# An expert-weight ring of 2 MB slots, and small matmuls packed in row and column groups, in a decoder step with 32 experts

## The reference

```
def moe(h, router_w, router_b, w_gu, b_gu, w_d, b_d):
    tok = h.reshape(-1, D_MODEL)
    logits = tok @ router_w + router_b
    top_v, top_i = lax.top_k(logits, TOP_K)            # 4 of 32 experts
    gates = scatter(softmax(top_v), top_i)             # (tokens, 32)
    for each expert:                                   # wgu 1024x2048, wd 1024x1024
        u = tok @ wgu + bgu
        glu = minimum(u[:, ::2], 7.0)
        lin = clip(u[:, 1::2], -7.0, 7.0)
        a = glu * sigmoid(1.702 * glu) * (lin + 1.0)
        acc += g[:, None] * (a @ wd + bd)
    return acc
```

## Time and profile before

| what | value |
|---|---|
| median of 3 runs | 1356.5 us (1354.03 to 1365.93) |
| span of the profiled execution | 1356.6 us |
| PE busy | 1267.8 us, 93% |
| VectorE / ScalarE / GpSimd busy | 317.1 / 256.0 / 67.5 us |
| moved by DMA | 500.45 MB, mean 369 GB/s |
| loads of w_gate_up | 256 of 1024 KB, 9.2 us from issue to landing (median) |
| loads of w_down | 128 of 1024 KB, 9.4 us |
| late constants | 1 of 288 KB, 11.6 us |

### The profile page before, as it was taken

The page is one execution under the profiler, slowest core; times in us unless marked ns, Lnnn a source line. Parts: engine busy times, 40 slices in busy tenths (PEclk is TensorE's granted clock), DMA queues, the critical chain, the costliest instruction groups (busy, mean ns, idle before and its releaser), DMA issues.

```text
span 1356.6 us, 20869 instructions
## 1 busy us (share of the span) xinstructions
PE 1267.8 (93%) x7744; PEld 606.1 (45%) x7744; DVE 317.1 (23%) x558; ACT 256.0 (19%) x573; POOL 67.5 (5%) x81
## 2 busy tenths in 40 slices
PE   7999988999799999999999999999999999999997
PEld 3588744454634343443434344343434344343433
DVE  1144525135411112211111122211111122111113
ACT  3143331222301011111201010211101011111102
POOL 2021003312000000000000000000000000000000
PEclk8999999999799999999999999999999999999999
DMA  9489978987889999999999999999999999999980
GB/s 338 171 316 353 338 251 295 354 305 226 332 329 405 413 411 415 418 415 417 415 417 409 411 419 414 419 415 416 409 417 413 415 420 416 419 403 416 415 340 36
DMA packets 120784, 500.45 MB, mean 369 GB/s; under 512 B 11925, under 2 KB 12074, under 8 KB 87946
## 3 DMA queue, kind: packets, MB, share of 16 engines
q1 hardware_dynamic: 117226, 488.03, 90.7%
q0 software_dynamic: 3520, 11.93, 2.5%
HBM read 495.20 MB, written 4.72 MB: 369 GB/s over the span
## 4 chain that ended last, share of the span: by engine, by line
PE 84%; DVE 5%; DMA 4%; issue 3%; ACT 3%; SPq 1%; POOL 0%; DVEq 0%; ACTq 0%; POOLq 0%
PE psum L838 32%; PE psum L865 17%; PE psum L798 7%; PE psum L424 6%; PE psum L411 5%; PE psum L813 5%; PE psum L827 4%; ACT arena L909 2%; PE psum L506 2%; SPq L386 1%; PE psum L549 1%; DVE arena L1496 1%; DMA arena<-cache_k 1%; DMA arena<-cache_v 1%; DMA arena<-x_sample 1%
## 5 line engine op out<-in xcount | busy, mean ns | idle before, releaser
L838 PE MATMUL psum<-arena 128*64 128x512 f32 x2048 | 445.3, 592 | 0.0
L838 PEld LDWEIGHTS psum<-arena 128*64 128x64 f32 x2048 | 161.0, 137 | 278.5 <-issue 278.5
L865 PE MATMUL psum<-arena 128*64 128x512 f32 x1024 | 226.8, 595 | 22.7 <-issue 11.7
L909 ACT ACTIVATE arena<-psum 128x512 f32<-128x512 f32 (+4 forms) x234 | 122.7, 545 | 532.7 <-PE psum L865 197.6
L1475 DVE TENSOR_SCALAR arena<-psum 128x512 f32<-128x512 f32 x32 | 22.1, 692 | 735.4 <-PE psum L838 735.4
L865 PEld LDWEIGHTS psum<-arena 128*64 128x64 f32 x1024 | 77.6, 137 | 151.3 <-issue 136.5
L813 PE MATMUL psum<-arena 128*128 128x512 f32 (+1 forms) x204 | 98.6, 612 | 25.6 <-DVE arena L1496 24.4
L1104 ACT ACTIVATE arena<-arena 128x512 f32<-128x512 f32 x32 | 20.1, 630 | 460.2 <-DVE arena L1475 460.2
L424 PE MATMUL psum<-arena 128*128 128x512 f32 x224 | 101.3, 610 | 3.4 <-DMA arena<-w_in 3.4
L411 PE MATMUL psum<-arena 128*128 128x128 f32 (+2 forms) x693 | 87.8, 279 | 15.1 <-DMA arena<-ret_norm_g 6.6
L798 PEld LDWEIGHTS psum<-arena 128*128 128x128 f32 x816 | 94.8, 196 | 14.2 <-issue 13.0
(11 more groups left out here) (195 smaller groups left out, 563.0 us busy)
## 6 DMA issues: line engine op xcount, KB each, us to landing
arena<-w_gate_up SPq DMA_DIRECT2D x256, 1024.0 KB, 9.2
arena<-w_down SPq DMA_DIRECT2D x128, 1024.0 KB, 9.4
arena<-cache_v SPq DMA_DIRECT2D x128, 256.0 KB, 5.1
arena<-cache_k SPq DMA_DIRECT2D x96, 256.0 KB, 5.8
arena<-w_in SPq DMA_DIRECT2D x7, 2048.0 KB, 10.7
arena<-cache_k POOLq DMA_DIRECT2D x32, 256.0 KB, 5.7
arena<-w_out SPq DMA_DIRECT2D x2, 2048.0 KB, 10.7
out<-arena POOLq DMA_DIRECT2D x1, 2048.0 KB, 13.5
```

Source lines behind the costliest of these rows:

```text
L838: last = mm(psum[64 * g:64 * (g + 1), b, :], xt[:, k, lhs], w[:, c:c + 512], start=False, stop=k == KC - 1, skip_group_check=True)
L865: last = mm(psum[64 * g:64 * (g + 1), 2, :], at_sb[:, q, SLOTS * half:SLOTS * (half + 1)], dn[:, m, 512 * g:512 * (g + 1)], start=m == 0, ...
L909: return nc.scalar.activation(out, in_, ACT.Copy, scale=scale)
```

## The change

The weights of an expert come in six parts of 2 MB, four of gate-up (256 rows each) and two of down (512 rows each). A part is laid out so that each partition holds 2 or 4 neighbouring rows of DRAM, one run of 16 KB. The parts go in turn through a ring of eight slots (16 MB), wherever their places lie in the arena (`PLACE`); one counter `w_used` releases them. To find room, the small buffers of the expert stage move to other regions. Since a partition now holds neighbouring rows, the gather picks every second column of the normed tokens, its gains come in a matching order through two more small transposes, and the transposes of the activation take every fourth column.

Four kinds of small matmuls are arranged anew. The bias table stands on 64 partitions, one half of each 1024 columns on 32 rows, and a bias matmul works on 32 rows and 64 columns of the array. The sample part of the combine becomes one unit of four matmuls of 32 columns and 256 elements into one bank, added to a buffer `y_quarters`, which is filled ahead of the loop and copied back after it. In the gather, the sample tile is kept twice, on partitions 0 to 31 and 32 to 63 (with its ranks), and its matmuls use 32 rows each, for two banks in turn. The last pair does not gather; pairs of the second loop gather for themselves. The first loads ahead of the loop are issued in another order. (Long blocks of removed lines are cut; they stand in the functions above.)

```diff
+RING = 8
+WSLOT = 4096
+PLACE = (0, 6, 7, 4, 5, 3, 1, 2)
+PARTS = 6
...
+    put("expert", np.tile(np.eye(E), (P // E, 1)))
...
-        gu = at(0, KC, F2)
+        gate_slot = [at(WSLOT * place, 2, F2) for place in PLACE]
+        down_slot = [at(WSLOT * place, 4, D) for place in PLACE]
-        dn = at(DN, KC, D)
...
-            pe.wait_ge(gains_in, 48)
-            transposes(V, [gain_in[0:20, :]], 20)
+            pe.wait_ge(gains_in, 64)
+            V.wait_empty(pe)
+            tr(psum[:, V.bank(), 0:20], gain_in[0:20, :], ident[0:20, 0:20])
+            for m in range(2):
+                last = tr(psum[:, V.bank(), 20 + 4 * m:24 + 4 * m], gain2_in[0:4, m::2], ident[0:4, 0:4])
+            V.filled(last)
...
-                for k in range(KC):
...
+                for kk in range(2):
+                    for m in range(2):
+                        for bank in range(2):
+                            cols = slice(512 * bank + 256 * kk + m, 512 * bank + 256 * (kk + 1), 2)
+                            o = psum[:, 6 + bank, P * (2 * kk + m):P * (2 * kk + m + 1)]
+                            for tile in range(2):
+                                mm(o, hn[:, tile, cols], sel[:, tile].rearrange("p a b -> p (a b)"),
+                                   start=tile == 0, stop=False, skip_group_check=True)
+                        for bank in range(2):
+                            cols = slice(512 * bank + 256 * kk + m, 512 * bank + 256 * (kk + 1), 2)
+                            o = psum[:, 6 + bank, P * (2 * kk + m):P * (2 * kk + m + 1)]
+                            rows = slice(NS * bank, NS * (bank + 1))
+                            last = mm(o, hn[rows, 2, cols], sel[rows, 2].rearrange("p a b -> p (a b)"),
+                                      start=False, stop=True, skip_group_check=True)
                 last.then_inc(xt_full, 1)

             def combine(m):

                 pe.wait_ge(sgt_ready, m + 1)
                 pe.wait_ge(out_ready, m * 2 + 1)
+                for u in range(4):
+                    tile, half = u // 2, u % 2
+                    if u >= 2:
+                        pe.wait_ge(comb_added, m * 5 + (u - 1))
+                    mm(psum[:, 3 + half, :], sgt[:, P * tile:P * (tile + 1)],
+                       out2[:, 512 * half:512 * (half + 1)], start=True, stop=True)\
+                        .then_inc(comb_full, 1)
+                pe.wait_ge(comb_added, m * 5 + 3)
+                for j in range(4):
+                    last = mm(psum[NS * j:NS * (j + 1), 3, 0:256], sgt[:, 2 * P:2 * P + NS],
+                              out2[:, 256 * j:256 * (j + 1)], start=True, stop=True)
+                last.then_inc(comb_full, 1)
+
+            def combine_last(m):
...
+                pe.wait_ge(comb_added, m * 5)
...
-            def pair(n, ahead):
-
-                pe.wait_ge(xt_ready, n + (1 if ahead else 2))
-                pe.wait_ge(esel_ready, n + (1 if ahead else 2))
+            def pair(n, landed, ahead):
+
+                pe.wait_ge(xt_ready, n + 1)
+                pe.wait_ge(esel_ready, n + 1)
                 for e in range(2):
                     pe.wait_ge(u_read, n * 2 + (e + 1))
                     lhs = slice(SLOTS * e, SLOTS * (e + 1))
-                    for b in range(2):
...
+                    for b, g in ((0, 0), (1, 1), (0, 1), (1, 0)):
+                        mm(psum[64 * g:64 * (g + 1), b, :], esel[E * b:E * (b + 1), e, :],
+                           bgu[E * b:E * (b + 1), g, :], start=True, stop=False, skip_group_check=True)
+                    for kk in range(4):
+                        slot, value = landed(PARTS * e + kk)
+                        pe.wait_ge(wt_in[slot], value)
+                        for m in range(2):
+                            for b in range(2):
+                                for g in range(2):
+                                    c = 1024 * g + 512 * b
+                                    last = mm(psum[64 * g:64 * (g + 1), b, :], xt[:, 2 * kk + m, lhs],
+                                              gate_slot[slot][:, m, c:c + 512], start=False,
+                                              stop=kk == 3 and m == 1, skip_group_check=True)
+                        last.then_inc(w_used, 1)
...
+                    for m in range(4):
+                        last = tr(psum[:, 5, P * m:P * (m + 1)], a_sb[:, m::4], ident)
                     last.then_inc(at_full, 1)
                     if e == 1:
-                        pe.wait_ge(comb_added, n * 6 + 6)
+                        pe.wait_ge(comb_added, n * 5 + 5)
...
-                    for m in range(KC):
...
+                    for q in range(2):
+                        slot, value = landed(PARTS * e + 4 + q)
+                        pe.wait_ge(wt_in[slot], value)
+                        for m in range(4):
+                            for g in range(2):
+                                last = mm(psum[64 * g:64 * (g + 1), 2, :],
+                                          at_sb[:, m, SLOTS * q:SLOTS * (q + 1)],
+                                          down_slot[slot][:, m, 512 * g:512 * (g + 1)],
+                                          start=q == 0 and m == 0, stop=q == 1 and m == 3)
+                        last.then_inc(w_used, 1)
+
+            pe.wait_ge(hn_copied, 1)
...
+            with pe.Fori(0, PAIRS // 2 - 1) as i:
+                pair(i * 2, in_turn(i, 0), True)
+                pair(i * 2 + 1, in_turn(i, 1), True)
+            pair(PAIRS - 2, in_turn(PAIRS // 2 - 1, 0), True)
+            pair(PAIRS - 1, in_turn(PAIRS // 2 - 1, 1), False)
...
+            act.wait_ge(hn_ready, 2)
+            copy(hn[NS:2 * NS, 2, :], hn[0:NS, 2, :]).then_inc(hn_copied, 1)
...
+            v.tensor_copy(rankm[NS:2 * NS, 2, 0:E], rankm[0:NS, 2, 0:E]).then_inc(rank_ready, 1)
+            dve.wait_ge(rank_ready, 2)
...
-                v.tensor_copy(esel, ident[:, bass.ds(first, 2)].unsqueeze(2).broadcast_to([P, 2, SLOTS]))\
+                v.tensor_copy(esel[0:2 * E], late_const("expert")[0:2 * E, bass.ds(first, 2)].unsqueeze(2)
+                              .broadcast_to([2 * E, 2, SLOTS]))\
...
+            def added(n):
+                for i in range(5):
+                    tile, half = i // 2, i % 2
+                    dve.wait_ge(comb_full, n * 5 + (i + 1))
+                    if i < 4:
+                        dst, got = y[:, tile, 512 * half:512 * (half + 1)], psum[:, 3 + half, :]
+                    else:
+                        dst, got = y_quarters, psum[:, 3, 0:256]
+                    v.tensor_tensor(dst, got, dst, ALU.add).then_inc(comb_added, 1)
...
+            dve.wait_ge(y_ready, 2)
+            for j in range(4):
+                v.tensor_copy(y_quarters[NS * j:NS * (j + 1), :], y[0:NS, 2, 256 * j:256 * (j + 1)])\
+                    .then_inc(quarters_ready, 1)
+            dve.wait_ge(quarters_ready, 4)
...
+            dve.wait_ge(comb_added, more * 5 + 5 * PAIRS)
+            for j in range(4):
+                v.tensor_copy(y[0:NS, 2, 256 * j:256 * (j + 1)], y_quarters[NS * j:NS * (j + 1), :])\
+                    .then_inc(quarters_ready, 1)
+            dve.wait_ge(quarters_ready, 8)
...
-            g_.memset(bgu, 0.0)
-            g_.memset(sgt, 0.0)
             link(g_.memset(out2, 0.0))
             pool.sem_inc(moe_zero, 1)
             pool.wait_ge(*mark["w_out"])
+            g_.memset(sgt, 0.0)
...
+            def load_part(e, part, slot):
+                if part < 4:
+                    src = w_gu[e] if isinstance(e, int) else w_gu[bass.ds(e, 1)].rearrange("a d f -> (a d) f")
+                    src, dst = src[256 * part:256 * (part + 1), :], gate_slot[slot]
                 else:
+                    src = w_dn[e] if isinstance(e, int) else w_dn[bass.ds(e, 1)].rearrange("a d f -> (a d) f")
+                    src, dst = src[512 * (part - 4):512 * (part - 3), :], down_slot[slot]
+                sp.dma_start(dst, src.rearrange("(p m) n -> p m n", p=P)).then_inc(wt_in[slot], 16)
+
+            def load_turn(t):
+                load_part(t // PARTS, t % PARTS, t % RING)

             sp.wait_ge(*mark["block6"])
+            load_turn(0)
             sp.wait_ge(rot_done, 2)
             sp.dma_start(rw, t["router_w"][0].rearrange("(k p) e -> p k e", p=P)).then_inc(router_in, 16)
             sp.dma_start(rb, t["router_b"][0:1].partition_broadcast(P).rearrange("p a e -> p (a e)"))\
@@ -1739,61 +1805,43 @@
             sp.dma_start(y[:, 0:2, :], x_p).then_inc(y_in, 16)
             sp.dma_start(y[0:NS, 2, :], x_s).then_inc(y_in, 16)
             sp.dma_start(f_gain, t["final_norm_g"].partition_broadcast(P)).then_inc(fg_in, 16)
+            sp.wait_ge(v_used, 32)
+            load_turn(1)
+            load_turn(2)
             sp.wait_ge(st2_ready, 1)
             sp.dma_start(late, t["shape_consts"][:, ncols:ncols + late_cols]).then_inc(late_in, 16)
+            sp.wait_ge(ret_ready, 1)
+            sp.wait_ge(*mark["vblk3"])
```

(72 more changed lines are left out.)

151 lines of the change are left out of this document (37 added, 114 removed).

## The result

| kernel | median | ratio to before |
|---|---|---|
| before | 1359.2 us (1354.03 to 1365.93, 4 runs) | 1 |
| changed | 1343.98 us (1341.97 to 1345.02, 4 runs) | 0.9887 [0.9866, 0.9908] |

The change makes the kernel 1.1% faster; a ratio of 1 lies outside the interval. The profiled execution spans 1343.2 us against 1356.6, 13.4 less; the forecast was 23 less. The rows are read in the order of those of before.

What follows compares the result with a forecast made beforehand. TensorE, busy 93% of the span, was taken as the bound, with DMA a few per cent behind. 1356.6 - 15.4 - 20.6 + 8.9 - 2.8 + 4.4 + 2.3 = 1333.4 us; own range 1322 to 1345, overall 1297 to 1376.

Steps and rivals of the forecast that it cites:

- Unit prices: TensorE: a full 512-column record takes 0.43 us, column groups overlap almost without loss, each change of array shape costs 0.19 us.
- Bias: 32 bias blocks, four matmuls at a time on 32 rows: 1.72 us becomes 1.24, gaining 15.4 us.
- Sample combine: Sample part of 16 combines, packed four matmuls at a time: 1.29 us saved each, gaining 20.6 us.
- Gather: 15 gathers in the loop: packing makes 5.55 us into 6.14, losing 8.9 us; the stride of two costs nothing.
- No last gather: Last pair: without its gather the transposes start when the activations are ready, gaining 2.8 us, not 5.55.
- Before the loop: Stretch ahead of the loop: first gather +0.9 us, copies on VectorE +1.2; sum +2.3, ends +1 and +8.
- DMA: Weight loads in 16 KB runs reach 427 GB/s; loop floor 914 us against about 945, so neither gain nor loss.
- rival D: Weight loads: 16 KB runs no faster, or worse; at 410 GB/s the floor of 951 us gives 1339; 7%.
- A: Bias and gather: row groups don't run side by side; bias loses 12.2 us, gather 22.8, total 1375; 17%.
- B: Bias and gather: shape changes cost nothing next to short records; weights become the bound, 1302 us; 13%.
- C: Gather and transposes: strided loads on TensorE take double, total 1412 us; 8%.
- E: The edits cancel: gather at its serial end, transposes doubled, bias as priced, total 1357 us; 10%.

Runs made afterwards that it cites:

- the unpacked pair of kernels: Changed kernel with gather unpacked, quarters' copies early and spare matmuls at the end, in 16 KB runs (ratio 0.977) and in 8 and 4 KB runs (0.9779).
- The spare matmuls: Changed kernel plus three unused 512-column matmuls in the last pair, where the last gather was: 1341.01 us, ratio 0.9856.
- the repeat: The changed kernel run again with no edit: 1345.02 us, ratio 0.9895.
- both row-group experiments: Changed kernel with bias matmuls on all 128 rows (1358.43 us), and with the gather's small matmuls all on rows 0 to 31 (1359.07 us).

## Why the prediction was right and where it was wrong

The direction and the mechanism held; the time, 1344 for 1333, lies at the top of the forecast's own range, 1322 to 1345, and 1 us above the 1343 under which the prediction would have said faster. (Against 1356.5, from which it reckoned, the ratio gives 1341.) A pair takes 59.33 us for the 59.3 forecast, but that match is in part luck: the gather with the transposes behind it costs 0.98 for 0.73, the bias gives 1.10 for 0.96, and the other transposes cost 0.05 for 0.14. By its steps:

**Unit prices: right.** The four small records of the gather's group take 0.43 us and lengthen the eight before them: 1.57 us a group, against 8 x 5.85/48 = 0.98 for full ones and 0.23 for the small ones. That leaves 0.36 for two changes of shape, 0.18 each; the forecast had 0.19.

**Bias: right in mechanism, 2 us better.** 0.55 us a block for 0.48. The forecast put the price of both changes on the bias; one is paid in the next block, in part.

**Sample combine: right**, 1.26 for 1.29; VectorE's wait stayed, 21.3 us before, 21.5 after.

**Gather: the mis-sized term.** "The gather's stride of two I take at nothing": it costs 0.26 us in the packed gather (6.29 against 6.03) and 0.30 in the unpacked (5.85 against 5.55), 4 us over the loop. VectorE's pass over every other element was no guide to TensorE's load. The rule of the Trainium skill (SBUF — State Buffer, on 16-byte lines) makes stride two free: in the unpacked pair of kernels it costs 0.006 us per load of 128x128 and stride four 0.0075 (0.44 to 0.47 for four), so these rows agree neither with "free" nor with a doubling. And the 0.68 us of the transposes is mostly a change of shape that the forecast had counted in the gather: contiguous it is 0.58 behind the packed gather, 0.44 behind the full one. The transposes' own stride was over-priced, 0.03 to 0.10 for 0.14. Over the loop: +14.7 for +11.0.

**No last gather: the gain was given back.** The transposes start 2.7 us sooner behind the gate-up block (2.89 for 5.55), with 2.8 forecast, and the down block 2.4. What the removed gather covered was named only for ScalarE, not for TensorE's clock: PE idles 2.9 us, and the down block takes 2.9 longer. The spare matmuls show it.

**Before the loop: +7.1 for +2.3, the largest miss.** The copies cost 1.2 as forecast. The stretch in which they stand grew by 2.1; most of the rest is that the counts behind the gather run at the low clock too (1.43 us; 0.80 in the repeat, where the clock had risen by then). The first gather was scaled from 8.02 us by the ratio of two gathers at full clock; it took 10.97 at 0.50 throughout, although PE was busy for 9.78 of the 10 us from 360 to 370, and the first gate-up block behind PE's wait 16.17 for 13.75. The row of 8.02 us already stood for a stretch at a clock of 0.72: a term of such a stretch needs its clock. What keeps the clock low there is not shown and stays open: the packed first gather took 10.3 to 11.0 us in six profiles with strides, but 8.2 in the one without, where the clock rose on the way; the unpacked ones took 8.1 to 8.5 in five. And a shorter first gather alone did not help the block behind it (16.35).

**DMA: right that it frees nothing, wrong about the old rate.** The 410 to 421 GB/s were what a pair of 60.65 us asks for, not what the queue can do: in runs of the same lengths it moves 418, so rival D's floor of 951 us was built on a demand. 427 GB/s for 16 KB was right: asked for 437, the transfers moved 425 to 430. A DMA share of 1.0 stood in every one of these kernels and tells none of them apart; the time from issue to landing does. It stays level where the transfers keep up (10.0 and 10.5 us in the changed kernel) and grows where they don't (14.3 and 28.5).

**Rivals.** A is excluded by both row-group experiments. B: a change does cost. C: strides cost a twentieth of the load, not double. D is partly true: the 16 KB runs brought nothing in the changed kernel. E, the edits cancelling, came about in part and from another side: 15 us of the 37 gained by bias and combine went to the gather, 10 to the clock at both ends and the copies.

## What to carry to other kernels

Packing by row groups pays where the packed block is long against two changes of shape (0.18 us each): eight 512-column records yes, four of 128 columns between full ones no. Before removing work that seems spare, see what it covers, the clock included, and price a stretch at low clock by its own rows. The rate of a ring that waits for its slots is the demand of the loop; its ceiling shows when the time from issue to landing grows through the loop.

## What the runs showed of the hardware

- A change of the array's shape between float32 blocks cost 0.16 us (bias, 0.31 for two) to 0.19 us; next to the gather's 128-column records it was 0.18.
- Two row groups run side by side even for 128-column records: 0.43 us for four records on two row groups, 0.67 on one.
- Behind a wait of PE of 2.9 us in the last pair the next block took 1.7 to 3.0 us longer (8.80 to 10.10 for 7.10, eight profiles), behind one of 1.3 us in the loop 1.7 (8.78 for 7.09, one profile). The length of one wait does not tell alone: in every pair PE also waits 1.5 us between units of the combine, and there the granted clock stayed at 1.00 (868.70 to 876.30 us) and the next down block at 7.09.
- Loads of weights with a stride of two words cost 0.26 to 0.30 us per 48, with a stride of four 0.03 per four.
- Asked for more (437 and 432 GB/s), the weight loads moved 425 to 430 GB/s in 16 KB runs and 418 in runs of 8 and 4 KB.
